# Prompt attention with the value blocks as the weights: both heads of a pair stream through, and the output comes turned

## The reference, cut to what matters

```python
def sparse_attend(q, kg, vg, valid):
    qg = q.reshape(Bn, Q, B_KV_HEADS, B_GROUP, HEAD_DIM)
    logits = jnp.einsum('bqgrd,bqkgd->bqgrk', qg, kg).astype(jnp.float32) * (HEAD_DIM ** -0.5)
    logits = jnp.where(valid[:, :, None, None, :], logits, -jnp.inf)
    p = jax.nn.softmax(logits, axis=-1).astype(vg.dtype)
    o = jnp.einsum('bqgrk,bqkgd->bqgrd', p, vg)
    return o.reshape(Bn, Q, B_HEADS * HEAD_DIM)
```

## Time and profile before

| | |
|---|---|
| median of 3 runs | 3950.78 us (3950.56 to 3956.41) |
| the profiled execution | 3949.73 us, of which the span from first to last instruction is 3948.1 us |
| TensorE / weight loads busy | 3519.9 us (89%) / 2741.8 us (69%) |
| VectorE, ScalarE, GpSimd busy | 2110.5 us (53%), 1030.8 us (26%), 507.9 us (13%) |
| granted TensorE clock, mean | 0.923 of full |
| chain that ended last | TensorE 73%, VectorE 6%, issue 6%, ScalarE 5%, DMA 4% |

### The profile page before, as it was taken

How to read it: one execution, slowest core, us unless ns; L and a number is a source line. 1 busy time by engine, 2 the same in 40 slices (tenths; PEclk the granted TensorE clock), 3 DMA queues, 4 the chain that set the end, 5 groups by cost and what they waited for, 6 DMA issues and landing times.

```text
span 3948.1 us, 54355 instructions
## 1 busy us (share of the span) xinstructions
PE 3519.9 (89%) x18810; PEld 2741.8 (69%) x18810; DVE 2110.5 (53%) x4861; ACT 1030.8 (26%) x2309; POOL 507.9 (13%) x667
## 2 busy tenths in 40 slices
PE   5888898978789999999987888898877899999999
PEld 3566566545548999999855566664555499999997
DVE  1346778787734443334323467788776433444444
ACT  2233323341521111111122333333425221111110
POOL 0111111021311000000001111111124110000000
PEclk9889989875899999999998999998759999999999
DMA  4122211236650111111320222211266411111111
GB/s 141 41 64 69 69 50 52 31 69 83 199 170 33 45 51 49 49 43 43 129 63 17 81 63 62 60 44 35 65 111 200 131 54 43 43 43 43 43 43 56
DMA packets 207768, 274.32 MB, mean 69 GB/s; under 512 B 74658, under 2 KB 160228, under 8 KB 207428
## 3 DMA queue, kind: packets, MB, share of 16 engines
q1 hardware_dynamic: 174836, 207.12, 18.8%
q0 software_dynamic: 25376, 52.89, 5.1%
q10 hardware_dynamic: 7280, 10.83, 0.8%
HBM read 245.16 MB, written 28.22 MB: 69 GB/s over the span
## 4 chain that ended last, share of the span: by engine, by line
PE 73%; DVE 6%; issue 6%; ACT 5%; DMA 4%; DVEq 1%; SPq 1%; POOL 1%; POOLq 1%; ACTq 0%; another core or an unknown queue 0%
PE bank L1508 13%; PE bank L1509 13%; PE bank L1510 13%; PE bank L1192 11%; PE bank L1188 5%; PE bank L1290 4%; PE bank L1502 3%; PE bank L1349 3%; ACT arena L788 2%; DMA arena<-in_w_out_strips 2%; PE bank L1274 1%; DVE arena L1573 1%; PE bank L1236 1%; PE bank L1424 1%; SPq L527 1%
## 5 line engine op out<-in xcount | busy, mean ns | idle before, releaser
L1980 DVE TENSOR_TENSOR x_rows<-x_rows,bank 128x512 f32<-128x512 f32 (+1 forms) x576 | 396.1, 688 | 633.2 <-PE bank L1510 633.2
L788 ACT ACTIVATE arena<-bank 128x512 f32<-128x512 f32 (+9 forms) x888 | 340.0, 438 | 966.4 <-PE bank L1192 327.2
L1192 PE MATMUL bank<-arena 128*128 128x512 f32 (+5 forms) x1440 | 525.2, 520 | 3.1 <-ACT arena L816 1.5
L1573 DVE TENSOR_SCALAR_CACHE_REDUCE arena<-arena,vectors 128x384 bf16<-128x384 f32 (+7 forms) x434 | 499.9, 1152 | 47.6 <-POOLq L429 15.6
L1508 PE MATMUL bank<-xT_hi,w_up_hi 128*128 128x364 f32 (+1 forms) x1536 | 505.4, 329 | 5.3 <-DVE vectors L1961 5.3
L1510 PE MATMUL bank<-xT_hi,w_up_lo 128*128 128x364 f32 (+1 forms) x1536 | 505.3, 329 | 0.0
L1509 PE MATMUL bank<-xT_lo,w_up_hi 128*128 128x364 f32 (+1 forms) x1536 | 505.3, 329 | 0.0
L1508 PE MATMUL bank<-w_down_hi,hidden_hi 128*128 128x512 f32 x1152 | 450.4, 391 | 7.5 <-issue 7.5
L1509 PE MATMUL bank<-w_down_lo,hidden_hi 128*128 128x512 f32 x1152 | 450.1, 391 | 0.0
L1510 PE MATMUL bank<-w_down_hi,hidden_lo 128*128 128x512 f32 x1152 | 449.7, 390 | 0.0
L1192 PEld LDWEIGHTS bank<-arena 128*128 128x128 f32 (+1 forms) x1440 | 253.6, 193 | 254.4 <-issue 225.8
(11 more groups left out here) (254 smaller groups left out, 4436.2 us busy)
## 6 DMA issues: line engine op xcount, KB each, us to landing
arena<-in_w_out_strips SPq DMA_DIRECT2D x80, 512.0 KB, 4.3
w_up_landing<-in_w_up SPq DMA_DIRECT2D x32, 1024.0 KB, 7.6
w_down_landing<-in_w_down SPq DMA_DIRECT2D x32, 1024.0 KB, 4.9
arena<-in_cache_k SPq DMA_DIRECT2D x160, 128.0 KB, 2.9
arena<-in_cache_v SPq DMA_DIRECT2D x160, 128.0 KB, 2.5
arena<-in_cache_v POOLq DMA_DIRECT2D x96, 128.0 KB, 2.9
arena<-in_cache_k POOLq DMA_DIRECT2D x96, 128.0 KB, 3.1
arena<-in_w_in ACTq DMA_DIRECT2D x4, 2048.0 KB, 16.1
```

The costliest lines, as they stand in the source:

```text
L788: return act.activation(dst, src, ACT.Copy, scale=scale)
L1192: ins = mm(b[:R, o:o + w], xnT[:, c, 0:R], w_in[:, c, c0:c0 + w], start=c == 0, stop=c == 7)
L1573: ts(junk, sc, cf[:R].bitcast(F32), None, ALU.is_ge, ALU.add, accum_out=cnt[:R])
L1980: tt(x, x, b[P - R:P, :], ALU.add).then_inc(s_took, 1)
```

## The change

- The probabilities are normalised before they are turned. VectorE inverts each head's sum after the first bit of the head's step (`invert_sum`; in the stages without a search of their own, after the step's bits), and ScalarE multiplies the row in place by the inverse (`normalise`), after the projection's copies of that step and ahead of `probs_out` of the head before. `probs_T` waits for that multiplication, not for the exponential.
- The turned probabilities of a pair of heads stand side by side (PTa, PTb, PTc), and `values` runs once for a pair, in steps 2, 4, 6 and 8: a block of V (128 keys x 64) is the weights, and the 256 columns of both heads' probabilities stream through. The output has the head's 64 dimensions on the partitions, as the output projection wants it.
- So the multiplication by the inverses at the end, its turn on TensorE and the buffer `yb` go. ScalarE copies bank 7 to `yB` in step 8 (`attention_out`).
- `head_max` waits for the turn of head h-2 (`turned_by_pe`), not for its values.
- Rows of the output projection's weights are reordered on the host to the new order of heads, and the sample attention writes in that order.

```diff
-        score, lg, PT, kq, el, S, h0s = zone(C0, E0, score=(3, SEQ), lg=(2, SEQ), PT=(1, 8, P), ...)
+        score, lg, PTa, kq, el, S, h0s = zone(C0, E0, score=(3, SEQ), lg=(2, SEQ), PTa=(4, 2, P), ...)
+        PTc = wq[:, 0, 0:4, :].rearrange("p (a b) c -> p a b c", a=2)
+        def turned_probs(q):
+            return (PTa[:, q] if q < 4 else PTb[:, q - 4] if q < 6 else PTc[:, q - 6])
@@ ScalarE
+                def normalise(t, h):
+                    act.wait_ge(s_inv, (l * NT + t) * 8 + h + 1)
+                    x = lg[:, h % 2, 0:width(t)]
+                    act.activation(x, x, ACT.Identity, scale=small[:, 88 + h:89 + h]).then_inc(s_pn, 1)
                 def probs_out(t, h):
+                    n = (l * NT + t) * 4 + h // 2
+                    if n >= 1:
+                        act.wait_ge(s_pv, n)
                     for k in range(0, t + 1, 4):
...
+                def attention_out(a):
+                    if l * (NT - EARLY) + max(a - EARLY, 0):
+                        act.wait_ge(s_ybst, l * (NT - EARLY) + max(a - EARLY, 0))
+                    act.wait_ge(s_pv, (l * NT + a + 1) * 4)
+                    copy(yB, bank[7][:, :].rearrange("p (c r) -> p c r", c=4)).then_inc(s_yb, 1)
@@ ScalarE, in the steps of a stage
-                        if h == 0 and attends(s - 1) is not None:
-                            (wait, take the bank of "yb", copy it to yB)
+                        if h < 8 and A_ is not None:
+                            normalise(A_, h)
                         if h >= 1 and A_ is not None:
                             probs_out(A_, h - 1)
+                        if h == 8 and A_ is not None:
+                            attention_out(A_)
@@ TensorE
                 def probs_T(t, h):
-                    pe.wait_ge(s_p, (l * NT + t) * 8 + h + 1)
+                    pe.wait_ge(s_pn, (l * NT + t) * 8 + h + 1)
...
-                def values(t, h):
-                    evac((l, t, f"pt{h}.{t // 4 * 4}"))
+                def values(t, c):
+                    evac((l, t, f"pt{2 * c + 1}.{t // 4 * 4}"))
+                    at = slice(64 * (c % 2), 64 * (c % 2) + 64)
                     for q in range(t + 1):
-                        ins = mm(bank[7][:, 64 * h:64 * h + 64], PT[:, 0, q, :], V[:, q, 64 * (h // 2):64 * (h // 2) + 64], start=q == 0, stop=q == t)
+                        ins = mm(bank[7][at, 256 * (c // 2):256 * (c // 2) + 256], V[:, q, 64 * c:64 * c + 64], turned_probs(q).rearrange("p g r -> p (g r)"),
+                                 start=q == 0, stop=q == t)
-                def attention_T(t):
-                    pe.wait_ge(s_yb, l * NT + t + 1)
-                    b = a_bank((l, t, "yb"))
-                    for c in range(4):
-                        ins = tr(b[:, c * P:(c + 1) * P], yb[:, c * P:(c + 1) * P], ident)
...
-                        if h >= 1 and A_ is not None:
-                            values(A_, h - 1)
+                        if h >= 2 and h % 2 == 0 and A_ is not None:
+                            values(A_, h // 2 - 1)
@@ VectorE
+                def turned_by_pe(t, h):
+                    v.wait_ge(s_full_a, A_AT[l, t, f"pt{h}.{t // 4 * 4}"] + 1)
+                def invert_sum(t, h):
+                    v.wait_ge(s_p, (l * NT + t) * 8 + h + 1)
+                    v.reciprocal(small[:, 88 + h:89 + h], small[:, 80 + h:81 + h]).then_inc(s_inv, 1)
                 def head_max(t, h):
-                    if q >= 2:
-                        v.wait_ge(s_pv, q - 1)
-                        v.wait_ge(s_p, q - 1)
+                    if h >= 2:
+                        turned_by_pe(t, h - 2)
+                    elif t:
+                        turned_by_pe(t - 1, h + 6)
...
-                            top_bits(sc, P, jk, left, left - BITS[h] + 1)
+                            top_bits(sc, P, jk, left, left)
+                            if A_ is not None:
+                                invert_sum(A_, h)
+                            top_bits(sc, P, jk, left - 1, left - BITS[h] + 1)
...
+                        if T_ is None and A_ is not None:
+                            invert_sum(A_, h)
...
-                    if A_ is not None:
-                        v.wait_ge(s_pv, (l * NT + A_) * 8 + 8)
-                        v.reciprocal(small[:, 88:96], small[:, 80:88])
-                        D_()
-                        tt(yb.rearrange("p (h d) -> p h d", h=8), bank[7][:, :].rearrange("p (h d) -> p h d", h=8),
-                           small[:, 88:96].unsqueeze(2).to_broadcast([P, 8, 64]), ALU.mult).then_inc(s_yb, 1)
+                    if A_ is not None and T_ is not None:
+                        turned_by_pe(A_, 7)
```

More of the change, by code:

```diff
@@ L102, in plan @@
                 if h == 0:
-                    if attends(s - 1) is not None:
-                        act.append((l, attends(s - 1), "yb"))
                     if projects(s) is not None:
@@ L401, in program @@
         s_idx = sem("relu_used")
-        s_nb, s_p, s_pv, s_yb = sem("max_ready"), sem("probs_ready"), sem("pv_done"), sem("yb_ready")
+        s_nb, s_p, s_pv, s_yb = sem("max_ready"), sem("exps_ready"), sem("pv_done"), sem("attention_out")
+        s_inv, s_pn = sem("sums_inverted"), sem("probs_normalised")
         s_out = sem("stored")
@@ L707, in _ @@
                         a = attends(s - 1)
-                        pool.wait_ge(s_evac, A_AT[l, a, "yb"] + 1)
+                        pool.wait_ge(s_yb, l * NT + a + 1)
                         store(y_part(a, 2, 4), yB)
@@ L983, in exp @@
                                    accum_out=small[:, 80 + h:81 + h]).then_inc(s_p, 1)
+                def normalise(t, h):
+                    act.wait_ge(s_inv, (l * NT + t) * 8 + h + 1)
+                    x = lg[:, h % 2, 0:width(t)]
+                    act.activation(x, x, ACT.Identity, scale=small[:, 88 + h:89 + h]).then_inc(s_pn, 1)
                 def probs_out(t, h):
+                    n = (l * NT + t) * 4 + h // 2
+                    if n >= 1:
+                        act.wait_ge(s_pv, n)
                     for k in range(0, t + 1, 4):
-                        m = min(4, t + 1 - k)
-                        g = (l * NT + t) * 8 + h
-                        if g >= 1:
-                            act.wait_ge(s_pv, g)
                         b = take((l, t, f"pt{h}.{k}"))
-                        copy(PT[:, 0, k:k + m, :], b[:, 0:m * P].rearrange("p (c r) -> p c r", c=m)).then_inc(s_evac, 1)
+                        for dst, at, top in ((PTa, 0, 4), (PTb, 4, 6), (PTc, 6, 8)):
+                            first, end = max(k, at), min(k + 4, t + 1, top)
+                            if first < end:
+                                ins = copy(dst[:, first - at:end - at, h % 2, :], b[:, (first - k) * P:(end - k) * P].rearrange("p (c r) -> p c r", c=end - first))
+                        ins.then_inc(s_evac, 1)
+                def attention_out(a):
[3 more added lines that the diff above has]
+                    copy(yB, bank[7][:, :].rearrange("p (c r) -> p c r", c=4)).then_inc(s_yb, 1)
                 def part_out(a, q):
@@ L1007, in _ @@
                     for h in range(9):
-                        if h == 0 and attends(s - 1) is not None:
-                            a = attends(s - 1)
-                            if l * (NT - EARLY) + max(a - EARLY, 0):
-                                act.wait_ge(s_ybst, l * (NT - EARLY) + max(a - EARLY, 0))
-                            b = take((l, a, "yb"))
-                            copy(yB, b[:, :].rearrange("p (c r) -> p c r", c=4)).then_inc(s_evac, 1)
                         if h < 8 and A_ is not None:
@@ L1356, in _ @@
                     for h in range(9):
-                        if h == 0 and attends(s - 1) is not None:
-                            attention_T(attends(s - 1))
                         if h == 1:
@@ L2025 @@
     arrays["in_consts"] = table
+    heads = arrays["in_w_out"][:, 256:768].reshape(DEPTH, 2, 2, 2, 64, DM).transpose(0, 1, 3, 2, 4, 5).reshape(DEPTH, 512, DM)
+    arrays["in_w_out"] = np.concatenate([arrays["in_w_out"][:, :256], heads, arrays["in_w_out"][:, 768:]], axis=1)
     arrays["in_w_out_strips"] = np.ascontiguousarray(arrays["in_w_out"].reshape(DEPTH, 8, P, 8, P).transpose(0, 3, 2, 1, 4))
```

12 lines of the change are left out of this document (5 added, 7 removed).

## The result

The changed kernel takes 3919.68 us, the median of four runs (3912.54 to 3922.78), beside 3953.60 for the kernel before in the same comparison. The ratio is 0.991, 95% interval 0.9891 to 0.9929. Its profiled execution takes 3917.89 us (span 3916.2), 31.8 less than that of before. 3928 was forecast; against the 23 us of the sum the profiled executions fell by some 9 us more.

A forecast was written before the change was run, and what follows sets the result against it. It took TensorE to lead, with waits for ScalarE's copies and half clock in tile 7. Terms -19 (tiles 0 to 5), -2, -5 and +3 summed to -23 us: 3928 us, own range 3915 to 3942, 80% over all 3902 to 3962.

The forecast's parts named there:

- Odd steps (-20): Tiles 0 to 5: 29 TensorE waits before values in steps 1, 3, 5, 7, 20.1 us together, go.
- The multiplication ahead of the copy (+17): Tiles 0 to 5, steps 2, 4, 6: ScalarE's new multiplication delays the copy TensorE waits for, costing 17 us.
- Matmul work (-9) and the turn of the output (-6): Tiles 0 to 5: paired 256-column value matmuls save 9 us; dropping the output's turn saves TensorE 6 us.
- VectorE holding back steps 0 to 2 (+3): Wider tiles: VectorE runs without a gap, exp(2) can't start earlier, so 3 us of TensorE's gain is given back.
- L1408's small waits (-4): Tiles 0 to 5, stage ends: TensorE's waits for VectorE, 3.6 us over twelve tiles, go, saving 4 us.
- The end of tile 5's stage and the start of tile 6's (-2): VectorE leads there; its wait for the last values goes, saving 2 us for both layers.
- the second rival: VectorE sets the stages' length and TensorE's gains only turn into waits: 3949 us, chance 0.14.
- Tile 6's stage (-5): VectorE's earlier release at its end and step 7 save, step 2's pair costs 2.5: 5 us less, both layers.
- Tile 7's stage (+3): TensorE bounds it at half clock; pairs of 17.7 us save 1 a layer, last pair costs 2.5: +3, both layers.
- the first: Rival: the low clock stays in the stages of tiles 6 and 7, slower, about 3967 us, chance 0.18.
- The third: Rival: the 256-column streams hold the clock up in tiles 6 and 7, pairs at 16 us: 3904 us, chance 0.15.
- The fourth: Rival: weight loads of the value matmuls are not hidden, 38 us more, 3966 us, chance 0.03.

The follow-up runs named there:

- the two unpaired kernels: The changed kernel with values run head by head, 128 columns each: 4023.39 us with the multiplication ahead of the copy, 3942.53 us with the copy ahead.
- the early inversion: The changed kernel with the inversion in tile 7's stage between the two search bits instead of behind them: 3926.60 us, ratio 0.9895.
- the kernel with both edits: The changed kernel with the copy ahead of the multiplication and tile 7's inversion between the two search bits: 3896.97 us, ratio 0.9825.

## Why the prediction was right, and where it was not

The sum had -23 us, and the stages show -33.0. Of the 10 us between them, 5 lie in tiles 0 to 5 (-19 forecast, -23.9 measured) and 4 in tile 7 (+3 and -1.4); tile 6 with the end of tile 5 was near (-7 and -7.7). In tiles 0 to 5 the terms for TensorE's work made -15 and those for its waits -4; its busy time fell by 24.0 us, and its idle time not at all.

**Odd steps (-20).** Right: the changed kernel has no value groups there. By the timeline, the waits of the even steps of tiles 0 to 5 grew from 61.2 to 76.6 us.

**The multiplication ahead of the copy (+17).** Right in mechanism, too small in size. The waits of the even steps grew by 15.4, and with the multiplication behind the copy they are 13.8 shorter. But the stages of tiles 0 to 5 then take 25.5 us less, half of it TensorE's busy time, and tile 6's 9.3 less. That the whole kernel gained only 21 to 22 is the 10.5 us that tile 7's stage lost to GpSimd's queue. The multiplication's own duration was a little low too: 396 ns for 128 columns and 1149 for 1024, where 310 and 1049 were taken from the earlier trace rows. Together they are 98.5 us by their rows, while ScalarE's busy time rose by 84.8.

**Matmul work (-9) and the turn of the output (-6).** The pitch is right: groups of 8, 10 and 12 take 1.94, 2.37 and 2.81 us at full clock, so 0.215 to 0.22 for each 256 columns, with the loads hidden. By the rule of the Trainium skill that was weighed ahead of the result (TensorE: Matmul & The Clock Gate, Part 3), these loads would show in the pitch; the trace doesn't bear that out. The term that was missing is the clock's. TensorE's busy time over the windows of tiles 0 to 5 fell from 1032.7 to 1008.7 us, against the -15 of the two terms that is 9 more, and its idle time is what it was, 161 us. The values and the turn took 7.5 and 6.0 us less, about as forecast. The input projections, whose work didn't change, took 14.0 less, and the other groups together some 4 more. The granted clock of the same windows gives the lower level 181 us before and 147 after (twice the share that is missing, times the length). Of the 24 us, 10 lie in tile 5 alone (106.81 to 98.88 in the first layer, 99.93 to 97.79 in the second), where the clock went from 0.87 and 0.92 to 0.94 and 0.95. The sum said "no change in the clock's share is counted elsewhere"; that is the step which failed in tiles 0 to 5, and it made the forecast too high.

That the lower level has a smaller share is not a chance of one run, though the place where it falls varies. The other nine paired kernels have it for 113 to 150 us in these stages, and the kernel before with only VectorE's wait changed has it for 195, with 0.94 and 0.89 in tile 5's stage. Nor is it the wide stream that holds the clock up: the two unpaired kernels have 137 us with the copy first and 205 with the multiplication first. The waits before the values don't order the kernels either: in tiles 0 to 5 the unpaired kernel with the copy first waits 83.9 us and the kernel before 81.3. What sets the share wasn't isolated and stays open.

**The low clock behind step 2's wait** is the same term seen close up. In step 2 ten matmuls took 4.50 in place of 2.37 us, with the clock at 0.50. The kernel before pays it as well, also at 0.50, but for one head's columns (2.40 for ten in the earlier trace rows, against 1.23 by the pitch of the earlier trace rows). So the change lost about 1 us more in tile 4's stage there, and something near it in each stage whose step 2 runs at the low clock.

**VectorE holding back steps 0 to 2 (+3), L1408's small waits (-4).** The run with only the new wait found nothing, so neither shows by itself; both were small. Of L1408's 3.6 us in tiles 0 to 5, 2.4 stay, all in tile 5's stage (L1420 now). The prediction also had no wait of the inversions for the exponentials in tiles 0 to 5. There are 16.7 us of it, 10.3 in tile 0, whose stages got shorter even so.

**The end of tile 5's stage and the start of tile 6's (-2).** TensorE's wait for VectorE's heads there grew from 14.2 and 12.7 us to 17.3 and 15.6: TensorE came earlier and VectorE did not. So some 6 us of what TensorE had won by then went into that wait, as the second rival has it.

**Tile 6's stage (-5).** Measured -7.7. The cause is the one named, the release at the end of the stage: putting that wait back made this tile's two stages 8.8 us longer, and TensorE's wait there went from 8.38 to 3.82, where 5 was forecast.

**Tile 7's stage (+3).** Measured -1.4, and here the premise was wrong, not the arithmetic. From maximum 0, 2 and 4 to the next but one it took 19.05, 17.95 and 17.79 us in the first layer (19.02, 19.76 and 17.83 before) where 17.7 was forecast; single pairs lie between 15.8 and 19.1. But "TensorE is the bound" holds of the steps, not of the stage. Its end is set by GpSimd's queue of stores and loads, which in the first layer ended 3 us ahead of the attention in the kernel before and 3 us behind it in the changed one, and in the second layer behind it in both. And with the clock at 0.68 the steps themselves are no longer TensorE's. The chain of inversion, multiplication and copy holds them: moving the inversion took 4.7 us off the eight maxima of a layer, and moving the copy ahead of the multiplication took off 4.1. One of the signs named for being wrong came true here: the turns waited 21.9 us for the multiplication in tile 7's stages, and 0.8 in all others. (VectorE was busy 76% of tile 6's stage before, but 74% of tile 7's, not 76% of both.)

**Of the rivals,** the first is refuted by the clock itself. The second is refuted by tiles 0 to 5: the stages shortened with VectorE's busy time unchanged (84.26 and 85.94 us in tile 4's). The third is half true: the clock did rise in the stages of tiles 6 and 7, but not because of the 256 columns, since the unpaired kernels with 128 have 0.71 to 0.73 in tile 7's stage. And the pairs of tile 7 were not 16 us on the whole, so its 12 us there didn't come. The fourth fell with the pitch.

**The best version** of the complete kernel has the copy first, the early inversion and the loads on SyncE: 3877.52 us, 2.2% under the kernel before. The version without the inversion's move is as good within the measurement.

## What to carry to other kernels

Work that is added to an idle engine costs by the instruction that it stands ahead of, not by its own length: the same 85 us of ScalarE cost 81 us more ahead of every awaited copy than behind it, and 22 more ahead of every second one. Behind the copies they cost nothing that shows in tiles 0 to 6, and in tile 7 some 9 to 10 us a layer, which another queue hid. Before costing the steps of a last stage, follow what the next part waits for through every queue, the stores of an idle engine among them; a stage can be full of busy engines and end on a store. And an unmodelled term to look for first is the clock: compare groups whose work did not change, and stage by stage, since time won in a stage that waits for something else is worth nothing.

## What the runs showed of the hardware

- Ten matmuls of 256 columns took 4.50 us behind a wait of 3.12 us, at a granted clock of 0.50, and 2.37 behind one of 1.35 us, at 1.00. The clock had fallen 1.8 us before the first of these waits began. In the unpaired kernel a wait of 1.33 us was also followed by the slow pace (2.37 for ten of 128 columns at 0.50, where others take 1.31), so the length of the last wait alone does not decide it.
- One kernel's clock falls in different places from layer to layer: in the kernel before with only VectorE's wait changed tile 5's stage has 0.94 and 0.89, and takes 112.1 and 119.4 us.
- GpSimd's sixteen stores of 1.5 KB each, with the three larger ones ahead of and between them, took 67 to 81 us from the first issue to the store behind them. In the first layer it was 75.3 in the kernel with both edits and 81.3 when the sixteen loads were moved to SyncE as well, which then ran beside them.
- Two kernels with the same matmuls but 85 us more or less of ScalarE's work had spans 1.1 us apart, with the difference in tile 7's stage hidden by a wait for another engine's queue.
